# A decoder layer's causal mask: laid on by VectorE with a minimum in the scores' banks instead of by products on TensorE

## What is computed

```python
def block(args):                      # q_blk: 128 queries, block j of 8
    q_blk, j = args
    s = jnp.einsum('bhcqd,bhckd->bhcqk', q_blk, k)      # c: the two softmaxes
    qpos = j * Q_BLOCK + jnp.arange(Q_BLOCK)
    mask = kpos[None, :] <= qpos[:, None]
    p = jax.nn.softmax(jnp.where(mask, s, -jnp.inf), axis=-1)
    a = p[:, :, 0] - lam * p[:, :, 1]
    return jnp.einsum('bhqk,bhkv->bhqv', a, v32)
```

## Time and profile before

| | us |
|---|---|
| median of 3 executions | 1958.7 |
| lowest and highest | 1956.92, 1960.9 |
| the profiled execution, its own time | 1959.85 |
| its span, first to last instruction | 1957.6 |
| TensorE busy | 1906.0 (97%) |
| VectorE busy | 1188.0 (61%) |
| ScalarE busy | 958.3 (49%) |
| GpSimd busy | 365.8 (19%) |

### The profile page before, as it was taken

The page is one execution under the profiler, slowest core; times in us unless marked ns, Lnnn a source line. Parts: engine busy times, 40 slices in busy tenths (PEclk is TensorE's granted clock), DMA queues, the critical chain, the costliest instruction groups (busy, mean ns, idle before and its releaser), DMA issues. The chain is left out here.

```text
span 1957.6 us, 25826 instructions
## 1 busy us (share of the span) xinstructions
PE 1906.0 (97%) x9314; PEld 1592.5 (81%) x9314; DVE 1188.0 (61%) x1538; ACT 958.3 (49%) x1618; POOL 365.8 (19%) x203
## 2 busy tenths in 40 slices
PE   6999999999999999999999999999999999999998
PEld 5788888888888888878888888878887888888886
DVE  6755666666665757543422122488777777789774
ACT  4355565656564655544434223226485665433341
POOL 1221212112121121212223444440000000121002
PEclk9999999999999999999999999999999999999999
DMA  4251514242423333252244434457576686564412
GB/s 168 89 172 55 178 55 157 74 150 86 148 88 123 107 101 134 72 173 67 81 158 144 156 119 159 174 192 269 201 273 235 211 295 223 187 235 146 155 65 86
DMA packets 91872, 291.77 MB, mean 149 GB/s; under 512 B 10872, under 2 KB 11640, under 8 KB 80784
## 3 DMA queue, kind: packets, MB, share of 16 engines
q1 hardware_dynamic: 89488, 282.31, 41.9%
q10 hardware_dynamic: 2304, 8.39, 1.1%
HBM read 203.56 MB, written 87.10 MB: 148 GB/s over the span
## 5 line engine op out<-in xcount | busy, mean ns | idle before, releaser
L708 PE MATMUL gp<-r1h,w_hi 128*128 128x512 f32 x1152 | 454.6, 395 | 2.2 <-POOL w_lo L1910 2.2
L710 PE MATMUL gp<-r1h,w_lo 128*128 128x512 f32 x1152 | 450.1, 391 | 0.0
L709 PE MATMUL gp<-r1l,w_hi 128*128 128x512 f32 x1152 | 449.5, 390 | 0.0
L1910 POOL TENSOR_TENSOR w_lo<-w_raw,w_hi 128x1024 fp32r<-128x1024 f32 x87 | 218.1, 2507 | 857.3 <-ACT w_hi L1036 857.3
L710 PEld LDWEIGHTS gp<-r1h,w_lo 128*128 128x128 f32 x1152 | 216.6, 188 | 46.4
L708 PEld LDWEIGHTS gp<-r1h,w_hi 128*128 128x128 f32 x1152 | 216.7, 188 | 45.4 <-POOL w_lo L1910 2.6
L709 PEld LDWEIGHTS gp<-r1l,w_hi 128*128 128x128 f32 x1152 | 216.9, 188 | 41.8
L956 PE MATMUL scores<-xh,qh 128*128 128x512 f32 x512 | 200.3, 391 | 3.2 <-ACT res L1309 2.3
L958 PE MATMUL scores<-xl,qh 128*128 128x512 f32 x512 | 199.2, 389 | 0.0
L960 PE MATMUL scores<-xh,ql 128*128 128x512 f32 x512 | 199.2, 389 | 0.0
L1158 ACT ACTIVATE pr<-scores,nb 128x256 f32<-128x256 f32 (+7 forms) x128 | 93.8, 738 | 117.8 <-DVE nb L1544 116.2
(11 more groups left out here) (327 smaller groups left out, 3698.2 us busy)
## 6 DMA issues: line engine op xcount, KB each, us to landing
xraw<-xo_d SPq DMA_DIRECT2D x54, 1024.0 KB, 5.4
w_raw<-in_in_blocks SPq DMA_DIRECT2D x64, 512.0 KB, 3.7
proj_d<-ev SPq DMA_DIRECT2D x128, 256.0 KB, 2.0
rq<-in_ff_quarters SPq DMA_DIRECT2D x32, 1024.0 KB, 8.0
xo_d<-res SPq DMA_DIRECT2D x78, 256.0 KB, 3.3
xo_d<-ring SPq DMA_DIRECT2D x60, 256.0 KB, 3.0
pr<-proj_d SPq DMA_DIRECT2D x16, 512.0 KB, 4.6
gt<-proj_d SPq DMA_DIRECT2D x32, 256.0 KB, 3.5
```

The costliest lines, as they stand in the source:

```text
L708: pe.matmul(gp[half][:], wh[slot][:, k, :], mh[:, k, t], start=(k == 0), stop=False)
L709: pe.matmul(gp[half][:], wh[slot][:, k, :], ml[:, k, t], start=False, stop=False)
L710: mm = pe.matmul(gp[half][:], wl[slot][:, k, :], mh[:, k, t], start=False, stop=(k == KT - 1))
L1910: pool.tensor_tensor(wl[slot][:], raw[slot][:], wh[slot][:].bitcast(F32), ALU.subtract).then_inc(w_split, 1)
```

## The change

The product with the mask table at L799 goes, and the scores' first product starts the accumulation in its place. The table becomes 128x128 in float32, with a very large negative number where a key is later than the query and 3e38 elsewhere. It is loaded from memory straight into `mask`; the identity in the rounded type, the casts and one memset of the prologue go. VectorE waits for each softmax's scores, and takes the minimum of the diagonal block and the table, in place in the scores' bank. A link of the chain stands behind the two minima, and then both row maxima follow. There are 8 more links in a head.

```diff
-        identr = sb("identr", [P, P], F32R, heads)
-        mask = sb("mask", [P, 3 * P], F32R, heads)
+        mask = sb("mask", [P, P], F32, heads)
...
-        DVE_HEAD = 46
+        DVE_HEAD = 54
...
-            sp.dma_start(sg[:, 0:3 * P], c_mask).then_inc(c2_in, 16)
+            sp.dma_start(mask[:], c_mask).then_inc(c2_in, 16)
...
-                        m0 = width - 2 * P
-                        moff = 0 if width == (i + 1) * P else P
                         for c in range(2):
                             for lo, hi in edges:
-                                diag = lo <= m0 < hi
                                 q = qs[:, c, i * P:(i + 1) * P]
-                                if diag:
-
-                                    pe.matmul(sp_[:, c, m0:m0 + 2 * P], identr[:], mask[:, moff:moff + 2 * P],
-                                              start=True, stop=False, skip_group_check=True)
-                                pe.matmul(sp_[:, c, lo:hi], q, ka[:, c, lo:hi], start=not diag, stop=False,
+                                pe.matmul(sp_[:, c, lo:hi], q, ka[:, c, lo:hi], start=True, stop=False,
                                           skip_group_check=True)
...
-            dve.memset(sg[:, 3 * P:], 0.0)
...
-            dve.tensor_copy(identr[:], ident[:])
-            pro.link(dve.tensor_copy(mask[:], sg[:, 0:3 * P]))
...
                     for c in range(2):
                         dve.wait_ge(s_done, 2 * (TT * h + i) + c + 1)
+                        d = sp_[:, c, i * P:(i + 1) * P]
+                        m = dve.tensor_tensor(d, d, mask[:], ALU.min)
+                    chain.link(m)
+                    for c in range(2):
                         m = dve.tensor_reduce(mx[:, c:c + 1], sp_[:, c, 0:(i + 1) * P], AX_X, ALU.max)
                     chain.link(m)
...
-    mask = np.zeros((P, 3 * P), np.float32)
-    mask[:, P:2 * P][np.arange(P)[None, :] > np.arange(P)[:, None]] = NEG
+    mask = np.where(np.arange(P)[None, :] > np.arange(P)[:, None], np.float32(NEG), np.float32(3e38))
```

## The result

| | before | changed |
|---|---|---|
| median, us | 1958.62 (4 executions) | 1970.75 (4 executions) |
| lowest and highest, us | 1956.92, 1960.9 | 1969.51, 1971.32 |
| the profiled execution, us | 1959.85 | 1971.15 |
| its span, us | 1957.6 | 1969.4 |
| TensorE, its products | 9314 | 9186 |

The ratio is 1.0059, with a 95% interval of 1.0046 to 1.0072: the change makes the kernel slower by 0.6%. The forecast was 1971 us. A fourth execution of the kernel before stands in this table, and brings its median from 1958.7 to 1958.62 us.

What follows compares the result with a forecast made beforehand. It took the head rounds' loop over VectorE, ScalarE and TensorE as the bound, despite TensorE's 97% busy. Seven rounds at +2.1 us give 14.6, less 1.9 in the last head: +12.7 on 1958.7, say 1971 us; range 1957 to 1982.

Steps and rivals of the forecast that it cites:

- a pair with its link: Two minima and a wait for VectorE's own result, per query tile: 0.53 us added to VectorE's work, bounds 0.42 and 0.64.
- exponentials late, tiles 0 to 3: ScalarE's exponentials in a head round against the trace before: +0, +0.53, +0.56 and +1.09 us.
- tiles 4 to 7: Lateness of the exponentials in the round's later tiles: +1.40, +1.40, +1.93 and +2.46 us.
- mLSTM's products of slot 11: TensorE's products that need tile 7's exponentials: slack 0.37 us, so +2.09 us; all later work moves with TensorE.
- a round: One of seven alike head rounds, 104.4 us before: 2.1 us longer, so 106.5 us; seven give 14.6 us.
- the last head: Eighth head, beside the gate columns: up to twice the matrix work, waits have slack, the full 1.9 us comes off.
- the faster rival: VectorE and ScalarE limit no slot; all removed TensorE products count: 15.1 us off, 1943.6 us; chance 0.11.
- The covers: Stalls hiding pairs: ScalarE's table load and evacuation at tile 0, nb's stalls behind GpSimd at tiles 2 and 5.
- the stall of nb: VectorE's negated maximum ends with GpSimd's operation: covers half a microsecond at tile 2, the whole pair at tile 5.
- the same walk: Tile-by-tile count of lateness through one head's VectorE, ScalarE and TensorE work: 2.1 us a round.
- the dearest of the rivals: Two new TensorE waits a round lower its clock: 24 us more, 1995 us; chance 0.09.
- The case of no change: A pair costs some 0.25 to 0.3 us, or another cover hides more: 1962 us at 0.27 us; chance 0.10.

## Why the prediction was right

The time was forecast at 1971 us and is 1970.75. The steps, one by one:

| step | forecast | measured |
|---|---|---|
| one minimum | 291 ns | 291 ns |
| a pair with its link | 0.53 us | 0.52 us |
| a link | 0.12 us | 0.12 us (two links: 0.40 in place of 0.52) |
| exponentials late, tiles 0 to 3 | 0, 0.53, 0.56, 1.09 | 0, 0.52, 0.55, 1.07 |
| tiles 4 to 7 | 1.40, 1.40, 1.93, 2.46 | 1.45, 1.44, 1.97, 2.49 |
| mLSTM's products of slot 11 | 2.09 | 2.12 |
| a round | 2.1 | 2.25 |
| seven rounds, from the table above | 14.6 | 15.9 |
| the last head | -1.9 | -1.0 |
| prologue and all behind the heads | 0 | -0.9 and -2.3 in the one pair of traces |

**The waits told more than the share of busy time.** TensorE's 97% spoke for the faster rival, and the run with the products out shows what they were worth: 2.9 us of 15.1. That the starts on TensorE stood right behind what they waited for the earlier trace rows was the right sign.

**The covers held.** Three tiles' pairs cost nothing, for the reasons given: the runs with tiles 0, 2 and 5 and with the others show it as a sum, the doubled pair shows how deep tile 2's cover is. That the stall of nb comes from GpSimd's operation is read from their common end. In the eleven traces, all 119 nb that start under an operation of GpSimd reaching beyond them end 0.02 to 0.03 us behind it, after 0.25 to 1.73 us; the other 585 take 0.17 us. GpSimd's operation was not moved by itself, so the cause is read from this agreement and not from an edit.

**The loop hands lateness on.** The doubled pair gave 0.92 us a tile in place of 0.52, and a round 4.64 us longer than before. This is the same walk with the other number, and holds it against any account by sums of busy time.

**Two terms were mis-sized, both the same way, and luck hid it.** A round is longer by 2.25 us and not 2.1: 0.05 us more at tile 4, of which 0.03 are left at the mLSTM's products of slot 11, and 0.13 us more behind those, where I held all work for tied to TensorE. Seven times that is 1.1 us. The last head gave back 1.0 us and not 1.9. The walk left it out with the words that its waits have slack; with the products out and no minima it is 1.8 us shorter, so the pairs cost 0.8 us there, and the doubled pairs 0.8 us more. One wait of 0.3 us is named in that stretch, for the low part of a tile. Rounds and last head together became 14.9 us longer, and the forecast had 12.7. That the time is still 1971 us is owed to the stretches ahead of the heads and behind them, 3.2 us shorter in this pair of traces, which no step of the walk had, and which no other trace ties to the change. The medians differ by 12.1 us.

**Two slips in the rivals.** By the walk's own terms a pair of 0.27 us makes a round 0.76 us longer, not 0.86, and the sign turns at 0.17 us a pair, not 0.13. Neither changes the forecast.

**The clock did not fall in the rounds.** From 130 to 880 us the granted clock of the changed kernel was 1.00, with waits up to 1.3 us in each round; over the whole span its mean is 0.998. The only low stretch in the heads is the one at the start of the last head (a PEclk of 0.66 from 880 to 885 us), the same as in the earlier trace rows:

```profile
880.00:885.00 5.00, 4.80 (x14) 3.84 (x15) 0.00 (x0) 0.00 (x0) 3.05 (x6) 0.66 0.74 218
```

So that case, the dearest of the rivals, is out by the profile. TensorE waits 2.2 us for GpSimd just before that stretch. In the traces with two links, with the convolution moved and with tiles 1, 3, 4, 6 and 7, the same wait of 2.2 us stands there and the clock stays at 1.00: the last of them has the changed kernel's rounds, and is 1.6 us shorter from slot 2 of the last round to slot 2 of the last head. So about that much of the difference between these traces and the changed kernel's stands outside the rounds. The case of no change is out too: the pair cost what the nearest row said.

## What to carry to other kernels

Before work is moved off the busiest engine, look at what each of its starts followed: where they stand right behind another engine's result, the removed work falls into the wait, and what the other engine gets in exchange is paid in full. Count the lateness tile by tile around the loop, and look for stalls that hide some of it; the same operation cost 0.4 to 0.5 us in each of five tiles and nothing in three. Move work where the trace shows cover, and give each operation that needs only one earlier result its own count instead of one link behind all.

## What the runs showed of the hardware

An operation of VectorE in place in a scores' bank took the same 291 ns as one that reads a bank and writes SBUF. A wait of VectorE for its own result cost 0.12 us against operations without one, and nothing of that is left when another operation is in flight meanwhile: two counts in place of one link brought the maxima from 0.52 to 0.40 us behind the pair's start. The same wait of TensorE, 2.2 us, was followed by a stretch at the lower clock in some traces and by none in three others. VectorE's operation of 128x2, 0.17 us by itself, lasted up to 1.73 us when it started under an operation of GpSimd, and then always ended 0.02 to 0.03 us behind it.
